# A hybrid decoder layer on one core: two dense steps moved ahead of the sliding-window attention, and the hi/lo split of two finished heads moved three steps earlier

## The reference, cut to what matters

```python
u = rms_norm(h, norm1_gain)
proj = u @ w_in                                   # 1024 x 2816
hq, hf, hi, hg, aq, ak, av = split(proj)
o_rec = hgrn2_mixer(hq, hf, hi, hg, lb, out_gain) # 4 heads, gated linear recurrence in chunks
o_att = swa_sink_mixer(aq, ak, av, ...)           # 8 query heads, 2 key heads, window 128, sinks
h = h + concat(o_rec, o_att) @ w_out
u = rms_norm(h, norm2_gain)
h = h + (silu(u @ w_gate) * (u @ w_up)) @ w_down  # d_ff 2816
```

## Time and profile before

| | |
|---|---|
| median of three executions | 1170.65 us |
| profiled execution | 1170.05 us |
| its span | 1168.2 us |
| PE busy | 1125.9 us (96%) |
| DVE busy | 705.1 us (60%) |
| ACT busy | 503.1 us (43%) |
| POOL busy | 445.4 us (38%) |

### The profile page before, as it was taken

The page is one execution under the profiler, slowest core; times in us unless marked ns, Lnnn a source line. Parts: engine busy times, 40 slices in busy tenths (PEclk is TensorE's granted clock), DMA queues, the critical chain, the costliest instruction groups (busy, mean ns, idle before and its releaser), DMA issues.

```text
span 1168.2 us, 14646 instructions
## 1 busy us (share of the span) xinstructions
PE 1125.9 (96%) x5540; PEld 927.0 (79%) x5540; DVE 705.1 (60%) x870; ACT 503.1 (43%) x773; POOL 445.4 (38%) x348
## 2 busy tenths in 40 slices
PE   7999999999999999889899999999999999999998
PEld 7988767788888788656788888888888877888876
DVE  7214598495869894659643333424243477777786
ACT  7314467535364631436333333333333354454532
POOL 0301134353342330210644544454536554343452
PEclk9999999999999999989999999999999999999999
DMA  7101100010104102320313331233213494545433
GB/s 271 37 1 54 37 19 20 19 37 19 36 19 158 55 2 95 120 78 19 128 55 125 117 118 62 109 118 117 102 70 126 162 343 154 178 124 177 134 96 149
DMA packets 37093, 112.63 MB, mean 96 GB/s; under 512 B 4896, under 2 KB 9760, under 8 KB 35616
## 3 DMA queue, kind: packets, MB, share of 16 engines
q1 hardware_dynamic: 37024, 111.71, 27.2%
HBM read 83.12 MB, written 28.57 MB: 96 GB/s over the span
## 4 chain that ended last, share of the span: by engine, by line
PE 79%; DVE 8%; ACT 4%; issue 4%; POOL 3%; DMA 1%; SPq 0%; DVEq 0%; ACTq 0%; POOLq 0%
PE ps L1241 23%; PE ps L1242 23%; PE ps L1243 23%; PE ps L1445 4%; PE ps L1404 1%; PE ps L1417 1%; DVE B L1778 1%; POOL D L715 1%; POOL sc L687 1%; PE ps L1256 1%; DVE olo L1636 1%; DVE M L1811 1%; DMA wraw<-wo_b 0%; DVE yacc L1951 0%; ACT ohi L872 0%
## 5 line engine op out<-in xcount | busy, mean ns | idle before, releaser
L1603 DVE TENSOR_TENSOR glo<-graw,ghi 128x1024 fp32r<-128x1024 f32 x21 | 26.2, 1246 | 147.4 <-POOL s34raw L634 147.4
L1241 PE MATMUL ps<-uhi,whi 128*128 128x512 f32 x272 | 112.1, 412 | 0.0
L1243 PE MATMUL ps<-uhi,wlo 128*128 128x512 f32 x272 | 106.4, 391 | 0.0
L1242 PE MATMUL ps<-ulo,whi 128*128 128x512 f32 x272 | 106.1, 390 | 0.0
L715 POOL TENSOR_TENSOR D<-B 128x1024 f32<-128x1024 f32 x28 | 64.8, 2314 | 42.5 <-DVE M L1811 23.4
L1951 DVE TENSOR_TENSOR yacc<-ps,yacc 128x512 f32<-128x512 f32 x104 | 68.8, 683 | 9.0 <-PE ps L1243 8.9
L1241 PE MATMUL ps<-ubhi,arhi 128*128 128x512 f32 x176 | 68.9, 392 | 2.3 <-DVE yacc L1951 2.2
L730 POOL TENSOR_TENSOR hst<-sg,up 128x512 f32<-128x512 f32 x21 | 29.1, 1384 | 103.7 <-issue 60.9
L1242 PE MATMUL ps<-ublo,arhi 128*128 128x512 f32 x176 | 68.5, 389 | 0.0
L1243 PE MATMUL ps<-ubhi,arlo 128*128 128x512 f32 x176 | 68.5, 389 | 0.0
L627 POOL TENSOR_TENSOR s12raw<-uraw 128x512 f32<-128x512 f32 x21 | 28.2, 1341 | 104.9 <-DVE rec L1862 61.4
(11 more groups left out here) (287 smaller groups left out, 3133.6 us busy)
## 6 DMA issues: line engine op xcount, KB each, us to landing
hidden<-hst SPq DMA_DIRECT2D x11, 1792.0 KB, 6.1
ubraw<-hidden SPq DMA_DIRECT2D x33, 512.0 KB, 5.4
graw<-wg SPq DMA_DIRECT2D x21, 512.0 KB, 4.3
uraw<-wu SPq DMA_DIRECT2D x21, 512.0 KB, 3.4
wraw<-wproj SPq DMA_DIRECT2D x17, 512.0 KB, 3.4
araw<-wd SPq DMA_DIRECT2D x22, 384.0 KB, 4.3
x<-xT SPq DMA_DIRECT2D x8, 512.0 KB, 6.8
h<-xT SPq DMA_DIRECT2D x8, 512.0 KB, 5.1
```

The lines of the kernel that those rows point to most:

```text
L1241: nc.tensor.matmul(out, whi_, xhi_, start=first, stop=False, skip_group_check=seeded)
L1242: nc.tensor.matmul(out, whi_, xlo_, start=False, stop=False, skip_group_check=seeded)
L1243: return nc.tensor.matmul(out, wlo_, xhi_, start=False, stop=last, skip_group_check=seeded)
L1603: nc.vector.tensor_tensor((glo2 if g == 2 else glo[g % 2])[:, :], graw[g % 2][:, :], ghi[g % 2][:, :].bitcast(F32), ALU.subtract).then_inc ...
```

## The change

All steps stay the same; only their order changes, in three lines.

```diff
@@ -109,13 +109,13 @@
-    order += mix(take(6), [[("AD", 4)], [("AM", 4)], [("AN", 4)], [("AH", 4)], [("AL", 4)]], lead=1)
+    order += mix(take(8), [[("AD", 4)], [("AM", 4)], [("AN", 4)], [("AH", 4)], [("AL", 4)]], lead=1)
...
-    order += mix(take(14), steps[:units]) + mix(take(4), steps[units:units + LAG])
+    order += mix(take(14), steps[:units]) + mix(take(2), steps[units:units + LAG])
@@ -172,9 +172,9 @@
             if h == NH - 2:
-                steps[5] += [("MS", 4)]
-                steps[6] += [("ML", 4), ("MS", 5)]
-                steps[7] += [("ML", 5)]
+                steps[2] += [("MS", 4)]
+                steps[3] += [("ML", 4), ("MS", 5)]
+                steps[4] += [("ML", 5)]
```

## The result

| | before | after |
|---|---|---|
| median of 20 executions | 1168.35 us | 1171.71 us |
| lowest, highest | 1166.85, 1170.92 | 1169.20, 1174.66 |
| profiled execution, its span | 1170.05, 1168.2 | 1173.14, 1170.9 |
| mean granted clock over the executions | 0.9962 (84 of them, from all comparisons) | 0.9938 (20) |

One further execution of before took 2284.4 us, in a slower state than all others, and is in none of these figures.

What follows compares the result with a forecast made beforehand. The prediction took time to be what TensorE waits for (79% of the chain). Moved dense steps +1.2 and sooner MS/ML steps -1.1 gave +0.1 us on 1170.65, so 1170.8 us, range 1168.0 to 1174.2.

Steps and rivals of the forecast that it cites:

- (a): Ahead of AM 4: a dense step moved there cuts the gap from 1.65 to 0.28, -1.4 us.
- (b): First attention steps: weight steps moved earlier make TR 2 and TR 3 later, +0.5 us, bounds 0 and +0.9.
- (c): Attention's end: no dense step left between TR 13 and TR 14, gap grows by 1.38, +1.4 us.
- (d): Start of H1: first sigmoid waits for ScalarE alone, TR 15 + 2.58; KT 0's gap grows from 1.41 to 2.1.
- Part one: Dense steps moved against the attention, effect up to KT 0: +1.2 us, bounds +0.4 and +1.9.
- Part two, the waits: MS/ML 4 and 5 three steps sooner: d2 waits for GpSimd, KT 3 loses its gap yet starts +0.5 us.
- R2: Head 3's d2 does not wait for GpSimd: -3.4 us there, whole kernel 1168.5 us; chance 0.20.
- Part two, the clock: Behind KT 3: the clock fall goes with its gap, none after the new gap at OC 2 6, -1.6 us.
- R1: Clock falls at new gaps of KT 0 and OC 2 6, 1.6 us each: 1174.0 us, one alone 1172.4; chance 0.25.
- R3: Moved dense steps only exchange gaps, 0 us; with -1.1 from the MS/ML steps 1169.5 us; chance 0.10.

Runs made afterwards that it cites:

- the filled pair: Kernels before and after, each with matmuls that nobody reads put into TensorE's gaps: medians 1166.83 us and 1168.04 us.
- part one alone: Kernel before with only the change's two take counts, the four MS/ML steps where they were: median 1171.78 us, ratio 1.0020.
- part two alone: Kernel before with only the four MS/ML steps three steps sooner, attention as before: median 1171.19 us, ratio 1.0020.
- the last two kernels of the table: Kernel before with ML 4 and ML 5 behind the last state and AM 4 one dense step later, without and with filling matmuls: 1164.90 and 1163.38 us.

## Why the prediction was right or wrong

**(a) AM 4: right.** Gap 0.29 (forecast 0.28). SC 0 at 142.60, 9.29 after AM 4 (forecast 142.35 - 133.02 = 9.33). No stall ahead of it.

**(b) The first attention steps: the mechanism right, the size not.** Forecast +0.5, bounds 0 and +0.9; measured TR 15's 2.51 less the dense step's 1.38 = 1.13. TR 2 is 1.51 late in this measure, TR 3 1.10, where 0.9 and 0.5 were forecast, 0.6 too little each. The step put the evacuation of P 12 3 "ahead of TR 2's copy". DVE's timeline of the kernel after shows it one copy sooner:
```profile
150.72 1.22 DVE L1670 TENSOR_TENSOR wlo<-wraw,whi 128x1024 fp32r<-128x1024 f32 x1
...
155.65 0.68 DVE L1701 TENSOR_TENSOR rawq<-ps,rs 128x512 f32<-128x512 f32 x1
156.25 0.68 DVE L1762 COPY pT<-ps 128x512 f32<-128x512 f32 x1
...
157.29 1.89 POOL L687 TENSOR_TENSOR sc<-sc,smax 128x1024 f32<-128x1024 f32 x1 [3.35 <-DVE smax L1755]
```
The copy at 156.25 is TR 1's, and GpSimd's scaling for TR 2 comes behind it at 157.29. The evacuation's 0.60 therefore fell on the very chain that TR 2 waits for. The list printed with the change says so (P 12 3, then PV 0, TR 1, SN 2): it was there to be read. The 0.60 is as large as what the forecast is short of, but that it is the cause is argued: with WL 7 put back 0.39 are left, and no run moves the evacuation alone.

**(c) The attention's end: right.** Two pauses around PV 13, 0.88 + 1.08 = 1.96 (forecast 2.0); TR 15's gap 0.68.

**(d) H1: right.** The table load is 1.30 behind TR 15 and the sigmoid 2.60 (forecast 2.58), no longer released by DVE's evacuation; from TR 15 to KT 0 22.21 us pass (forecast 22.2). KT 0's gap is 2.14 (forecast 2.1). Part one in sum: +1.87 against +1.2, nearly the whole difference from (b), at the upper bound of +1.9, which the prediction had for "a late evacuation more".

**Part two, the waits: right.** d2 of head 3 took 2.74 (forecast 2.7), the gap at OC 2 6 is 2.06 (forecast 2.3), KT 3 starts without one, +0.53 in the filled pair ((405.50 - 239.21) - (403.30 - 237.54); forecast +0.5). ML 5's own wait of 1.7 came too. The rule of the Trainium skill that the prediction weighed ("SBUF — State Buffer", "SBUF: two separate sides", the port pair of VectorE and GpSimd is held by one instruction at a time) is borne out by d2's 2.74, and, with the order turned round, by 1.22 for d2 and 3.22 for X. R2, that d2 doesn't wait, is refuted.

**Part two, the clock: wrong, and the larger error.** The step took -1.6 us because the fall behind KT 3's gap would go with the gap. Its size was about right (1.2 to 1.4 us between KT 3 and O 40 0), and it is common: it is there in four of the five profiles that have the gap. What failed is that its going was booked as a gain with all else left as it was. The kernel with the low parts behind the state has no gap at KT 3 either; it gains its 2.5 us of wait and nothing beside it, and its executions lose as much to the clock as those of before (4.6 and 4.5), in its profile behind the 4.1, behind the 3.18 at 563, and at 972. In the change itself the fall came back in two places: behind KT 0's new gap and behind O 40 0, an old gap for which the prediction quoted full speed, 2.2 us in both profiles. The base was also a poor one: the profiled execution had a mean clock of 0.994, as low as in only 12 of 84 executions of before (mean 1170.8 us); 7 have 0.999 (mean 1167.1).

**R1, the clock falls at the new gaps: half right.** The prediction's own sign of being wrong, a fall near 238, came. The clock fell at KT 0 in both profiles of the kernel after and with WL 7 put back, not in part one alone; at OC 2 6 in part two alone, not in the two profiles of the kernel after. Its price was too high for KT 0, whose transposes take 1.90 instead of 1.09 while a later wait hides a part of the loss: in part one alone, with no fall there, TensorE waits 0.59 for DVE at 255.06, and in the kernel after that wait is gone. KT 3 is 272.69 after AM 4 with that fall and 272.23 without, 0.5 us. R1 had put it at 1.6. The forecast total of R1 for one fall, 1172.4, is near the measured one, but not by its reasons: the dear fall was at an old gap, and its base was 2.3 too high. R3, that the P's only exchange gaps, is refuted by +1.87 at KT 0.

**The sum.** Forecast: waits +1.2 + 0.5 = +1.7, clock -1.6. Measured: waits +2.4, and +2.9 in all. By the granted clock after loses 2.8 us more than before (7.3 to 4.5), which would be +5.2 if each lost microsecond cost one. The measured total says less, and within the executions of before the seven at 0.999 and the twelve at 0.994 or less differ by 3.7 us in time and at least 5.8 in loss, some 0.6 for one. Even so 2.4 + 1.7 is about 1 more than measured; with means in place of medians the difference is 3.1. The mean loss has steps of 1.2 us an execution, and each median is uncertain by some tenths. Three things stay open: this 1 us; why the fall behind O 40 0 goes with either part of the change (six of six profiles against none of five, and the mean losses with them, shown as a coincidence and not as a mechanism: the gap and the instructions around it are the same, its moment is not); and what a lost microsecond costs. Filling gives it back one for one in before (-2.1 for -2.1), but in after only 3.6 for 6.1 (+2.9 to -0.7), 0.6 for one; between the last two kernels of the table it is 2.2 by the ratios, or 1.5 by the medians, for 2.7. How often each gap is followed by a fall within one kernel was not measured: two profiles are too few.

## What to carry to other kernels

Waits that engines set for one another repeated from one profile to the next within 0.1 us at the places compared here (a late load can still add one, as the 1.10 at 450.96), clock falls didn't: keep the two in separate sums, and don't book a fall's going as a gain, since an old gap elsewhere can start to cost it. When an instruction is moved past a load on the same engine, write down for each moved DVE instruction which copy or reduction now stands behind it; the forecast here was 0.6 us short at a step where it had one evacuation a place too late in the list. A low part that only has to be there later goes behind the state update that TensorE waits for, not ahead of the chain that feeds it; and where TensorE must wait, matmuls that nobody reads can keep its clock at 2.4 GHz.

## What the runs showed of the hardware

- An idle stretch of TensorE of the same length was followed by a fall of the granted clock or not. Ahead of KT 0 (2.13, 2.14): three falls in four profiles. OC 2 6 (2.06, 2.07): one in three. KT 3 (2.24 to 2.34): four in five. O 40 0 (2.42 to 2.44): six in eleven. The first gate product (4.1): eleven in eleven. The gap of 3.2 some 60 us behind it: eleven in fourteen. It also fell behind 1.91 (at 972, low parts behind the state) and 1.78 (at 1140, after), and not behind 2.29 (at 973, AM 4 later).
- The price of a fall depends on what follows: 0.5 us at KT 0, 1.2 to 1.4 at KT 3, 2.2 at O 40 0 where it lasted longer and 0 to 0.4 where it ended sooner.
- 25 filling matmuls, in stretches in which TensorE would have waited anyway, took 1.5 us off the median (1164.90 to 1163.38) and brought the spread from 3.9 us over ten executions to 1.8 over five.
- When DVE and GpSimd both have instructions of two SBUF inputs ready, they alternate, and each stands for the other's length: d2 2.74, GpSimd's difference 2.75, ML 5 2.91, in a row.
